# Sixteen rotating homes for the expert weights of a mixture-of-experts layer, with a staging buffer that VectorE fills

## The chip, the cores and the metric

The kernel runs on one core of one Trainium2 chip. The metric is the device time of one execution in microseconds (us). TensorE (PE in the profile) multiplies, VectorE (DVE) and ScalarE (ACT) work element by element, GpSimd (POOL) gathers and scatters rows by indirect DMA, SyncE (SP) issues the weight loads.

## The reference, cut to what matters

One layer of an encoder trunk: a matrix-memory branch and a latent-attention branch, merged, then a top-4-of-32 mixture of experts on 336 tokens of 1024 features, all in float32. The change lies in the mixture of experts:

```python
def moe(x2, w_router, b_router, w_gu, b_gu, w_dn, b_dn):
    logits = (x2 @ w_router).astype(jnp.float32) + b_router.astype(jnp.float32)
    top_v, top_i = lax.top_k(logits, TOP_K)
    gates = jax.nn.softmax(top_v, axis=-1)
    ...
    def expert_block(args):
        xb, e = args
        gu = xb @ w_gu[e] + b_gu[e]
        gate = jnp.minimum(gu[:, :D_FF], SWIGLU_LIMIT)
        up = jnp.clip(gu[:, D_FF:], -SWIGLU_LIMIT, SWIGLU_LIMIT)
        hid = (up + 1.0) * gate * jax.nn.sigmoid(SWIGLU_ALPHA * gate)
        return hid @ w_dn[e] + b_dn[e]
```

An expert's weights are 1024 x 2048 (gate and up) and 1024 x 1024 (down), together 12 MB. All 32 experts get tokens, so all 384 MB are read once.

## The kernel before, in words

The first 584 us do the two branches, the output projection and the router; the change only renames buffers there. From then on the kernel works in blocks of 64 token rows, each of one expert. With the given inputs there are 39 blocks: experts 8, 10, 18, 20 and 29 have two, expert 26 has three, the other 26 have one.

An expert's weights come as 12 pieces of 128 x 2048 float32 (1 MB): `up 0` to `up 7` (gate and up columns for 128 input rows each) and `down 0` to `down 3`. Each piece has a fixed place in the buffer `ring` (`up_w`, L360; `dn_w`, L369), so there is room for exactly one expert. SyncE loads them in a loop over experts (L568 to L577): piece k of the next expert is issued when TensorE has used piece k of this expert in this expert's last block (semaphores `m_up`, `m_down`; each piece's landing is counted in `up_in[k]`, `dn_in[j]`).

TensorE's loop (L1084 to L1103) is skewed by a block. An iteration b turns the tokens of block b+1 (L619, eight transposes), adds the biases (L1015), turns the hidden rows of block b (L619, four), and then takes the twelve pieces in the order up 0 (of block b+1), down 0, 1, 2 (of block b), up 1, down 3, up 2 to up 7 (L1025, L1031 are gate and up, L1051 is down). Each piece is four matmuls of 64 rows by 512 columns, each of which the profile lists as two. A pair, left columns then right columns, runs side by side in the two column halves of the array. VectorE's loop (L1848 to L1863) does the gated unit between up 7 and the turning of the hidden rows: clip gate (L1440), `pick` for the bias (L1440), clip up (L1440), multiply (L1443), `hid` (L1446). ScalarE does the sigmoid and the copies out of PSUM. GpSimd gathers the token rows (L1973) and scatters the results (L2001) for each block; down 0 of a block waits until the scatter of the block before has landed (`yrow_free`).

After the last block the twelve result pieces `y_turn` are loaded into `ring` and summed (L588 on).

Of the kernel before, what the change touches and what calls it, by code (L numbers as in the profile page):

```python
# [22 lines left out]
D = 1024  # L23
# [73 lines left out]
UPSLOT, DNSLOT = [4, 5, 3, 0], [1, 2]  # L97
# [103 lines left out]
def build(nc, i, o, x_rows_dram, y_rows_dram):  # L201
    with ExitStack() as ctx:
# [7 lines left out]
        ring = sb("ring", [128, 6 * SLOT])  # L210
        r_xt = sb("r_xt", [128, KD * NT])
        r_o = sb("r_o", [128, KD * NT])
        r_kv = sb("r_kv", [128, 3968])
        r_qk = sb("r_qk", [128, 16 * (NT + 3)])
        r_v = sb("r_v", [128, KD * NT])
# [5 lines left out]
        u_pad = sb("u_pad", [128, 2, NT + 6])  # L221
        sig = sb("sig", [128, 2, NT + 3])
# [9 lines left out]
        wrow = sb("wrow", [4, 2, NT])  # L232
        emat = sb("emat", [128, 2, NT])
        wib_hi = sb("wib_hi", [128, 2, NT])
# [5 lines left out]
        def r3(ap, a):  # L240
            return ap.rearrange("p (a b) -> p a b", a=a)

        ident = cst("ident")
        scratch = ring[:, 4 * SLOT:6 * SLOT]
# [7 lines left out]
        bd_rows = r_v[0:NE, 0:1024]  # L252
# [3 lines left out]
        oT = r3(ring[:, 3 * SLOT:3 * SLOT + KD * NT], KD)  # L256
# [46 lines left out]
        g_ffn_b = r_v[:, 1216:2240]  # L303
        g_fin_b = r_xt[:, 0:1024]
        w_rt = r3(r_xt[:, 1024:1280], KD)
# [38 lines left out]
        inslot = r3(r_kv[:, 0:12 * BLK], 12)  # L344
        inblk = r3(r_kv[:, 1536:1536 + 12 * NB1], 12)
        spread = r3(r_o[:, 384:384 + 12 * NB1], 12)
        prod = r_o[:, 0:384].rearrange("p (t k e) -> p t k e", t=3, k=4)
        cmp6 = r_v[:, 2240:2240 + NE * 6].rearrange("p (e n) -> p e n", n=6)

        xg = r3(r_kv[:, 0:512], 8)  # L350
        hidT = r3(r_kv[:, 512:1024], 4)
        gt = r_kv[:, 1024:1536]
        up = r_kv[:, 2048:2560]
        sg = r_o[:, 0:512]
        gateT = r_o[0:NE, 2048:2048 + NT]
        hid = r_v[:, 0:512]
        xrow = r_v[0:BLK, 1216:2240]
        yrow = r_xt[:, 1280:1792]

        def up_w(k):  # L360
            at = UPSLOT[k // 2] * SLOT + 2 * D * (k % 2)
            return ring[:, at:at + 2 * D]

        def y_turn(t, r):
            n = 3 * r + t
            at = 4 * SLOT + D * n if n < 8 else 3 * SLOT + D * (n - 8)
            return ring[0:ROWS[t][1], at:at + D]

        def dn_w(j):  # L369
            at = DNSLOT[j // 2] * SLOT + 2 * D * (j % 2)  # L370
            return ring[:, at:at + 2 * D].rearrange("p (s f) -> p s f", s=2)
# [19 lines left out]
        def taken(eng, *name):  # L391
# [8 lines left out]
            "ld_w_q", "xg_even", "xg_odd", "sq_odd", "sq_sum", "x_var", "x_root", "xt_ready"))  # L400
        ld_cache, ld_x1, ld_C, stored_kv = sem("ld_cache"), sem("ld_x1"), sem("ld_C"), sem("stored_kv")
# [30 lines left out]
        def pslot(slot, n):  # L432
            return ring[:, slot * SLOT:slot * SLOT + n]
# [42 lines left out]
        dn = i["w_down"][0].rearrange("e (j p s) f -> p e j (s f)", p=128, s=2)  # L476

# [4 lines left out]
        def _(sp):  # L482
# [65 lines left out]
            sp.dma_start(bd_rows, i["b_down"][0]).then_inc(ld_late, 16)  # L548
            for k in range(4):
                sp.dma_start(up_w(k), gu[:, 0, k, :]).then_inc(up_in[k], 16)  # L550
# [7 lines left out]
            sp.dma_start(g_fin_b, i["g_final_norm"].rearrange("(a d) -> a d", a=1).broadcast_to([128, D])  # L558
                         ).then_inc(ld_late, 16)
            filled(sp, "ya", 7)  # L560
            for k in range(4, 8):
                sp.dma_start(up_w(k), gu[:, 0, k, :]).then_inc(up_in[k], 16)
# [1505 lines left out]
```

## Time and profile before

| | us |
|---|---|
| median of three runs | 1660.77 (1659.41 to 1665.76) |
| the profiled execution's own time | 1667.29 |
| its span | 1665.5 |
| TensorE busy | 1524.4 (92%) |
| VectorE busy | 360.3 (22%) |
| ScalarE busy | 339.8 (20%) |
| GpSimd busy | 131.7 (8%) |
| granted TensorE clock, mean | 0.951 |

The busy shares are averages over the whole span. From 584 us on the DMA engines read weights at 410 to 420 GB/s in most of the page's 40 slices, with dips in some, and TensorE is busy 80 to 99% of a slice. So the experts' part has to be read in stretches: where TensorE waits for a weight piece, and where the DMA queue has nothing to do.

### The profile page before, as it was taken

The page shows a single profiled execution, that of the slowest core. Times are in us where ns is not written, and L with a number is a line of the kernel's source. Part 1 is how long each engine was busy: PE and PEld are TensorE (multiplying, and loading weights), DVE is VectorE, ACT ScalarE, POOL GpSimd, SP SyncE. Part 2 cuts the span into 40 slices and gives each one's busy share as a digit, 9 for nine tenths or more (in the row PEclk, how much of TensorE's full clock was granted, in tenths as well). Part 3 has the DMA queues.
Part 4 walks back from the last instruction along what each step waited for, and adds up shares of the span by engine and source line. Part 5 has one row for each costly group of instructions (what it writes and reads, how often), then busy time and mean ns, then how long its engine had stood idle before and what let it go on. Part 6 is the DMA issues. An engine that isn't in the chain of part 4 may idle for free.

```text
span 1665.5 us, 20381 instructions
## 1 busy us (share of the span) xinstructions
PE 1524.4 (92%) x7060; PEld 698.1 (42%) x7061; DVE 360.3 (22%) x860; ACT 339.8 (20%) x648; POOL 131.7 (8%) x237
## 2 busy tenths in 40 slices
PE   9999999999999998877899988788999887998994
PEld 6666666666665433222233332222333222333331
DVE  4664522423201511010011100100111010101015
ACT  4434323534101111110111111101111110111111
POOL 1100000000000000000001100000101000010010
PEclk9998999999999999988999998889999998999996
DMA  9121132212554389999989899999899999579897
GB/s 346 62 80 65 54 110 78 77 51 102 172 205 168 136 319 414 417 419 408 418 311 403 361 414 415 410 411 421 306 374 388 408 414 398 237 310 413 331 410 263
DMA packets 91398, 478.91 MB, mean 288 GB/s; under 512 B 12490, under 2 KB 15386, under 8 KB 41952
## 3 DMA queue, kind: packets, MB, share of 16 engines
q1 hardware_dynamic: 82976, 462.15, 69.8%
q0 software_dynamic: 8096, 16.04, 2.9%
q8 instruction: 22, 0.36, 0.1%
q10 hardware_dynamic: 288, 0.22, 0.1%
q14 instruction: 16, 0.13, 0.0%
HBM read 472.81 MB, written 15.51 MB: 293 GB/s over the span
## 4 chain that ended last, share of the span: by engine, by line
PE 73%; DMA 18%; DVE 4%; issue 3%; SPq 1%; ACT 1%; DVEq 0%; POOLq 0%; POOL 0%; ACTq 0%
PE bank L615 28%; PE bank L1025 21%; DMA ring<-in_w_gate_up 17%; PE bank L1051 17%; PE bank L619 2%; PE bank L1031 1%; DVE r_kv L1443 1%; DVE r_v L1446 1%; PE bank L874 1%; PE bank L642 1%; DVE r_c L1446 1%; SPq L569 0%; PE bank L748 0%; DVE r_qk L1440 0%; SPq L576 0%
## 5 line engine op out<-in xcount | busy, mean ns | idle before, releaser
L1025 PE MATMUL bank<-ring,r_kv 128*64 128x512 f32 x2184 | 517.6, 621 | 89.1 <-DMA ring<-in_w_gate_up 88.5
L1025 PEld LDWEIGHTS bank<-ring,r_kv 128*64 128x64 f32 x2184 | 156.3, 142 | 396.5 <-issue 301.4
L1051 PE MATMUL bank<-ring,r_kv 128*64 128x512 f32 x1248 | 292.5, 612 | 0.7 <-ACT r_kv L1135 0.7
L1440 DVE TENSOR_SCALAR r_kv<-bank 128x512 f32<-128x512 f32 x78 | 53.9, 692 | 916.3 <-PE bank L1031 916.1
L615 PE MATMUL bank<-r_xt,ring 128*128 128x336 f32 x768 | 227.6, 451 | 1.1 <-ACT r_o L1135 0.9
L1051 PEld LDWEIGHTS bank<-ring,r_kv 128*64 128x64 f32 x1248 | 93.4, 144 | 197.7 <-issue 196.6
L615 PEld LDWEIGHTS bank<-r_xt,ring 128*128 128x128 f32 x768 | 144.1, 191 | 70.7 <-issue 5.7
L1135 ACT ACTIVATE r_xt<-bank 128x512 f32<-128x512 f32 x39 | 23.3, 597 | 509.7 <-PE bank L1051 509.7
L1386 ACT ACTIVATE r_o<-r_kv 128x512 f32<-128x512 f32 x39 | 24.6, 631 | 318.4 <-DVE r_kv L1440 318.4
L615 PE MATMUL bank<-ring 128*128 128x336 f32 (+2 forms) x352 | 87.6, 432 | 0.0
L619 PEld LDWEIGHTS bank<-const,r_v 64*128 64x128 f32 (+3 forms) x524 | 49.3, 156 | 77.3 <-DVE r_v L1446 43.9
L619 PE MATMUL bank<-const,r_v 64*128 64x64 f32 (+3 forms) x524 | 63.8, 257 | 10.8 <-DVE r_v L1446 10.4
L1031 PE MATMUL bank<-ring,r_kv 128*64 128x512 f32 x312 | 73.5, 592 | 0.0
L1135 ACT ACTIVATE r_kv<-bank 128x512 f32<-128x512 f32 (+3 forms) x85 | 49.8, 586 | 92.7 <-PE bank L619 87.4
L615 PEld LDWEIGHTS bank<-ring 128*128 128x128 f32 (+2 forms) x352 | 57.1, 189 | 26.8 <-issue 2.8
L615 PE MATMUL bank<-ring,r_kv 128*128 128x128 f32 (+4 forms) x192 | 60.0, 449 | 1.2 <-DVE r_kv L1443 1.2
L1386 ACT ACT_TABLE_LOAD x39 | 50.0, 1283 | 12.6 <-ACT r_xt L1135 12.4
L1997 POOL COPY r_qk<-r_qk 128x1 uint32 x39 | 7.0, 180 | 557.1 <-ACT r_xt L1135 557.1
L1015 PE MATMUL bank<-bgu,r_qk 32*64 32x512 f32 x312 | 42.4, 612 | 9.1 <-DVE r_kv L1440 8.8
L615 PE MATMUL bank<-r_kv,ring 128*128 128x336 f32 (+9 forms) x192 | 44.4, 360 | 0.0
L1973 POOL DMA_INDIRECT r_v<-x_rows,r_qk x41 | 40.0, 976 | 47.3 <-POOL r_qk L1990 33.2
L615 PEld LDWEIGHTS bank<-ring,r_kv 128*128 128x128 f32 (+3 forms) x192 | 30.9, 186 | 29.1 <-issue 23.6
(251 smaller groups left out, 945.7 us busy)
## 6 DMA issues: line engine op xcount, KB each, us to landing
ring<-in_w_gate_up SPq DMA_DIRECT2D x256, 1024.0 KB, 18.0
ring<-in_w_down SPq DMA_DIRECT2D x128, 1024.0 KB, 14.9
ring<-in_w_in SPq DMA_DIRECT2D x12, 2048.0 KB, 7.7
ring<-in_w_proj_b SPq DMA_DIRECT2D x2, 2048.0 KB, 7.6
ring<-in_w_proj_a SPq DMA_DIRECT2D x2, 2048.0 KB, 9.3
ring<-in_w_out SPq DMA_DIRECT2D x2, 2048.0 KB, 7.7
ring<-y_rows SPq DMA_DIRECT2D x8, 512.0 KB, 8.7
ring<-in_first SPq DMA_DIRECT2D x4, 592.0 KB, 5.8
```

The source lines that it names most:

```text
L615: ins = pe.matmul(out, l, r, start=(n == 0), stop=(n == len(pairs) - 1), **kw)
L619: return pe.transpose(out, src, ident[0:src.shape[0], 0:src.shape[0]])
L642: ins = pe.matmul(low[n][:, 0:NT], w_first[:, k, 128 * n:128 * n + 128], xg_mix[:, k, :], start=(k == 0), stop=(k == KD - 1), skip_group_c ...
L1015: pe.matmul(half(gate_bank if q < 2 else up_bank, q % 2), pick[32 * q:32 * q + 32, :], bgu[32 * q:32 * q + 32, :], start=True, stop=False, ...
L1025: ins = pe.matmul(half(gate_bank if q < 2 else up_bank, q % 2), xg[:, k, :], w[:, 512 * q:512 * q + 512], start=False, stop=False, skip_gr ...
L1031: ins = pe.matmul(half(bank_, t), xg[:, 7, :], w[:, 512 * (q0 + t):512 * (q0 + t) + 512], start=False, stop=True, skip_group_check=True)
L1051: ins = pe.matmul(half(out_bank, t), hidT[:, 2 * (j % 2) + s, BLK * h:BLK * h + BLK], w[:, s, 512 * t:512 * t + 512], start=(j == 0 and s ...
L1135: return act.activation(out, src, ACT.Copy, scale=scale)
L1386: act.activation(sg, gt, ACT.Sigmoid, scale=ALPHA).then_inc(m_sig, 1)
L1440: return dve.tensor_scalar(out, a, s1, s2, op0, op1)
L1446: return dve.scalar_tensor_tensor(out=out, in0=a, scalar=s, in1=b, op0=op0, op1=op1)
L1973: pool.indirect_dma_start(xrow, None, x_rows_dram[:, :], bass.IndirectOffsetOnAxis(ap=column[0:BLK, :].bitcast(U32), axis=0), bounds_check ...
```

## The change

`ring` now has sixteen homes of one piece each instead of fixed places for twelve. Piece n of expert e (up 0 to 7 are 0 to 7, down 0 to 3 are 8 to 11) lies at home (12 e + n) mod 16, so the pattern repeats every four experts. SyncE's loop over experts is written out for four phases. A piece may be issued when the piece sixteen places earlier in the stream has been used: `up 0` to `up 3` of expert e wait for `down 0` to `down 3` of expert e-2, `up 4` on for `up 0` on of expert e-1. Each load also waits for the landing of the same piece of the expert before. Four pieces of expert 1 are issued before the block table is ready. The room comes from buffers of the first part (`r_xt`, `r_v`, `r_o`), whose later tenants move to `usig`, `rowt`, `r_qk`, `r_c` and `r_rt`.

Because a piece's home differs from expert to expert and TensorE's loop is one body for all blocks, the matmul on the left 512 columns reads its weights through a register; the right columns (1024 elements a partition and piece) are copied by VectorE from the home into one of four fixed buffers `stage`, and the other matmul reads there. TensorE waits for the copy (`staged`) in place of the landing; VectorE waits for the landing and, from the fifth copy of an iteration on, for TensorE's use of the piece four uses earlier.

```diff
-UPSLOT, DNSLOT = [4, 5, 3, 0], [1, 2]
+PIECE, HOMES = 2048, 16
+USE = [("up", 0), ("down", 0), ("down", 1), ("down", 2), ("up", 1), ("down", 3)] + [("up", k) for k in range(2, 8)]
+def home(e, n):
+    return (12 * e + n) % HOMES
...
+        def experts_of(eng, b):
+            e, e1 = (eng.value_load(bei[0:1, bass.ds(eng.snap(b + n), 1)].bitcast(I32), min_val=0, max_val=NE - 1)
+                     for n in (0, 1))
+            def four(expert, n):
+                return ring[:, bass.ds(eng.snap((3 * expert + n) % 4 * (4 * PIECE)), 4 * PIECE)]
+            return (None, None, four(e, 2)), (four(e1, 0), four(e1, 1)), e, e1
...
             for j in range(4):
-                sp.dma_start(dn_w(j).rearrange("p s f -> p (s f)"), dn[:, 0, j, :]).then_inc(dn_in[j], 16)
+                down_in(0, j, dn[:, 0, j, :])
+            for k in range(4):
+                if k == 2:
+                    filled(sp, "lg", 2)
+                sp.wait_ge(up_in[k], 16)
+                gate_up_in(1, k, gu[:, 1, k, :])
+            sp.wait_ge(x2_ready, 3)
+            sp.dma_start(g_fin_b, i["g_final_norm"].rearrange("(a d) -> a d", a=1).broadcast_to([128, D])
+                         ).then_inc(ld_fin, 16)
             sp.wait_ge(moe_tab, 1)
-            with sp.Fori(1, NE) as e:
-                before = sp.value_load(firsti[0:1, bass.ds(e, 1)].bitcast(I32), min_val=0, max_val=MAXB)
-                for k in range(8):
-                    sp.wait_ge(m_up, before * 8 + k + 1)
...
+            def expert_in(e, phase, first_k=0):
+                old, before = last_block(e - 2) if first_k == 0 else None, last_block(e - 1)
+                for k in range(first_k, 8):
+                    if k < 4:
+                        sp.wait_ge(m_down, old * 4 + k + 1)
+                    else:
+                        sp.wait_ge(m_up, before * 8 + k - 3)
+                    sp.wait_ge(up_in[k], 16 * e)
+                    gate_up_in(phase, k, gu[:, bass.ds(e, 1), k, :].rearrange("p a f -> p (a f)"))
                 for j in range(4):
+                    sp.wait_ge(m_up, before * 8 + j + 5)
+                    sp.wait_ge(dn_in[j], 16 * e)
+                    down_in(phase, j, dn[:, bass.ds(e, 1), j, :].rearrange("p a f -> p (a f)"))
...
+            def moving(fours, n, u):
+                w, s = fours[n // 4][:, PIECE * (n % 4):PIECE * (n % 4) + PIECE], stage[:, u % 4, :]
+                return [lambda g: w[:, 1024 * g:1024 * g + 512], lambda g: s[:, 512 * g:512 * g + 512]]
...
-                gate_up(0, e1)
...
+                for u, (kind, n) in enumerate(USE):
+                    if u == 1:
+                        pe.wait_ge(m_hidT, b + 1)
+                        pe.wait_ge(yrow_free, b + 1)
+                    pe.wait_ge(staged, 12 * b + u + 1)
...
+            def stage_right(b, u, own, new, e, e1):
+                kind, n = USE[u]
+                if kind == "up":
+                    dve.wait_ge(up_in[n], 16 * e1 + 16)
+                    src = new[n // 4]
+                else:
+                    dve.wait_ge(dn_in[n], 16 * e + 16)
+                    src = own[2]
+                if u >= 4:
+                    was, m = USE[u - 4]
...
+                src = r3(src[:, PIECE * (n % 4):PIECE * (n % 4) + PIECE], 4)[:, 1:4:2, :]
+                dve.tensor_copy(r3(stage[:, u % 4, :], 2), src).then_inc(staged, 1)
...
+            with dve.Fori(0, last) as b:
+                glu(b)
+                own, new, e, e1 = experts_of(dve, b)
+                for u in range(12):
+                    stage_right(b, u, own, new, e, e1)
```

How the instructions stand now. TensorE before, from the turning of the hidden rows to down 0 (L619 is the turn, L1025 is up 0, L1051 down 0; ISA is a register instruction):

```order
L619 MATMUL bank1<-const,r_v 128x128 [waits m_hid]
L619 MATMUL bank1<-const,r_v 128x128 x3
L1021 ISA [waits m_xg]
L1025 MATMUL bank2<-ring,r_kv 64x512 [waits up_in0]
L1025 MATMUL bank2<-ring,r_kv 64x512
L1025 MATMUL bank3<-ring,r_kv 64x512 x2
L1046 ISA [waits yrow_free,m_hidT]
L1051 MATMUL bank4<-ring,r_kv 64x512 [waits dn_in0]
L1051 MATMUL bank4<-ring,r_kv 64x512 x3
```

The same place now (L665 is the turn, L1070 up 0, L1104 down 0):

```order
L665 MATMUL bank1<-const,r_qk 128x128 [waits m_hid]
L665 MATMUL bank1<-const,r_qk 128x128 x3
L1151 ISA [waits m_xg]
L1070 ISA [waits staged]
L1070 MATMUL bank2<-ring,r_qk 64x512
L1070 MATMUL bank2<-stage,r_qk 64x512
L1070 ISA
L1070 MATMUL bank3<-ring,r_qk 64x512
L1070 MATMUL bank3<-stage,r_qk 64x512
L1151 REGISTER_ALU [waits yrow_free,m_hidT]
L1104 ISA [waits staged]
L1104 MATMUL bank4<-ring,r_qk 64x512
```

The matmuls are the same in number and order; each piece has gained two or three register instructions, and its wait is for the copy. VectorE's loop before, from the multiply to the loop's end (L1443 the multiply, L1446 `hid`):

```order
L1443 TENSOR_TENSOR r_kv<-r_kv,r_o 128x512 [waits m_gt,m_sig]
L1446 SCALAR_TENSOR_TENSOR r_v<-r_kv 128x512 [waits m_dve,m_read]
L1861 REGISTER_ALU [waits m_hid]
L1848 REGISTER_ALU [waits moe_tab,m_pick]
L1848 COMPARE_AND_BRANCH
```

The same place now, up to the second copy (L1496 the multiply, L1499 `hid`, L489 reads the two expert numbers, L1931 the copies):

```order
L1496 TENSOR_TENSOR r_qk<-r_qk 128x512 [waits m_gt,m_sig]
L1499 SCALAR_TENSOR_TENSOR r_qk<-r_qk 128x512 [waits m_dve,m_read]
L489 ISA
L489 TENSOR_LOAD r_qk
L489 ISA x3
L489 TENSOR_LOAD r_qk
L489 ISA x2
L1919 ISA
L1931 ISA [waits up_in0]
L1931 COPY stage<-ring 128x1024
L1922 ISA
L1931 ISA [waits dn_in0]
```

Two register loads, nine register instructions and twelve copies now stand behind `hid` in every iteration.

## Rows read from the trace of the kernel before

**Rows 1.** The page: share of the span of the chain that ended last.

```profile
PE 73%; DMA 18%; DVE 4%; issue 3%; SPq 1%; ACT 1%; DVEq 0%; POOLq 0%; POOL 0%; ACTq 0%
```

**Rows 2.** Timeline of TensorE: start, length; in brackets idle before and releaser.

```profile
626.06 1.89 PE L1031 MATMUL bank<-ring,r_kv 128*64 128x512 f32 x8
627.88 0.71 PE L619 MATMUL bank<-const,r_v 64*128 64x64 f32 x8
...
630.14 0.74 PE L619 MATMUL bank<-const,r_v 128*128 128x128 f32 x4 [0.23 <-DVE r_v L1446]
630.81 1.94 PE L1025 MATMUL bank<-ring,r_kv 128*64 128x512 f32 x8
632.58 5.32 PE L1051 MATMUL bank<-ring,r_kv 128*64 128x512 f32 x24
...
649.75 1.89 PE L1031 MATMUL bank<-ring,r_kv 128*64 128x512 f32 x8
...
1018.64 3.68 PE L1025 MATMUL bank<-ring,r_kv 128*64 128x512 f32 x8 [6.35 <-DMA ring<-in_w_gate_up]
1022.11 6.37 PE L1051 MATMUL bank<-ring,r_kv 128*64 128x512 f32 x24
...
1143.35 3.68 PE L1025 MATMUL bank<-ring,r_kv 128*64 128x512 f32 x8 [6.08 <-DMA ring<-in_w_gate_up]
```

**Rows 3.** TensorE's waits in 640 to 820, 970 to 1150, 1300 to 1415, 1520 to 1545.

```profile
PE bank L1025 <- DMA ring<-in_w_gate_up: 31.9, 6, 6.7
...
PE bank L1025 <- DMA ring<-in_w_gate_up: 31.2, 6, 6.7
...
PE bank L1025 <- DMA ring<-in_w_gate_up: 20.7, 4, 6.6
...
PE bank L1025 <- DMA ring<-in_w_gate_up: 4.8, 1, 4.8
```

**Rows 4.** Stretches: busy of each engine, granted clock, DMA share, GB/s.

```profile
940.00:980.00 40.00, 39.54 (x198) 13.74 (x194) 4.17 (x8) 6.21 (x8) 3.77 (x6) 1.00 1.02 418
...
1450.00:1490.00 40.00, 39.07 (x200) 13.84 (x198) 5.67 (x10) 5.53 (x8) 3.94 (x6) 1.00 0.59 230
```

**Rows 5.** Timeline of VectorE: `hid`, before the turning.

```profile
629.39 0.69 DVE L1446 SCALAR_TENSOR_TENSOR r_v<-r_kv 128x512 f32<-128x512 f32 x1
```

**Rows 6.** Register loads and register work on the queues: ns min/median/max, first and last start.

```profile
L1085 PEldq TENSOR_LOAD <-r_qk x38: 298/302/319, 600.0 to 1601.6; - x38
L1085 PEldq FUSED_REGOPS  x38: 151/151/156, 600.4 to 1601.9; - x38
L1846 DVEq TENSOR_LOAD <-r_qk x1: 546/546/546, 600.5 to 600.5; - x1
L1440 DVEq FUSED_REGOPS  x39: 57/57/65, 603.5 to 1628.4; - x39
```

**Rows 7.** Groups of VectorE by shape: busy us, mean ns | idle before.

```profile
L1446 DVE SCALAR_TENSOR_TENSOR r_c<-ring,r_qk,r_c 128x1024 f32<-128x1024 f32 x8 | 10.3, 1284 | 9.6 <-DMA ring<-y_rows 9.6
...
L1440 DVE TENSOR_SCALAR ring<-ring,st 128x576 f32<-128x576 f32 x4 | 2.1, 520 | 0.1
...
L1440 DVE TENSOR_SCALAR ring<-ring,st 128x144 f32<-128x144 f32 x4 | 1.2, 296 | 0.1
```

**Rows 8.** Timeline of TensorE: the first block, and the last.

```profile
582.58 0.71 PE L619 MATMUL bank<-const,r_v 64*128 64x64 f32 x8 [0.48 <-DMA r_v<-x_rows,r_qk]
583.97 1.94 PE L1025 MATMUL bank<-ring,r_kv 128*64 128x512 f32 x8 [0.69 <-ACT r_kv L1135]
...
1631.39 0.93 PE L619 MATMUL bank<-const,r_v 128*128 128x128 f32 x4 [1.55 <-DVE r_v L1446]
1633.02 9.85 PE L1051 MATMUL bank<-ring,r_kv 128*64 128x512 f32 x32 [0.69 <-ACT r_kv L1135]
```

**Rows 9.** GpSimd's gather: its place in the timeline, and issue to landing of all.

```profile
630.20 0.98 POOL L1973 DMA_INDIRECT r_v<-x_rows,r_qk  x1 [0.86 <-POOL r_qk L1990]
...
DMA to landing us min/median/max: 3.0/7.0/8.9
```

More of the change, by code:

```diff
@@ L207, in sem, with r3 @@
             return ctx.enter_context(nc.semaphore(name))
[L210 to L213, printed above, removed]
+        def r3(ap, a):
+            return ap.rearrange("p (a b) -> p a b", a=a)
+        ring = sb("ring", [128, HOMES * PIECE])
+        spare = ring[:, 12 * PIECE:HOMES * PIECE]
+        r_xt, r_v, r_o = (spare[:, KD * NT * n:KD * NT * (n + 1)] for n in range(3))
+        stage = sb("stage", [128, 4, 1024])
+        r_kv = stage[:, :, :].rearrange("p a b -> p (a b)")[:, 0:3968]
         r_qk = sb("r_qk", [128, 16 * (NT + 3)])
-        r_v = sb("r_v", [128, KD * NT])
+        r_rt = sb("r_rt", [128, 256])
         r_c = sb("r_c", [128, 4112])
@@ L578, in _ @@
+            expert_in(1, 1, 4)
+            expert_in(2, 2)
+            expert_in(3, 3)
+            with sp.Fori(0, NE // 4 - 1) as n:
+                for phase in range(4):
+                    expert_in(sp.snap(4 * n + 4 + phase), phase)
             nb = sp.value_load(nbi[0:1, 0:1].bitcast(I32), min_val=NE, max_val=MAXB)
@@ L1017, in bias, with gate_up @@
                               start=True, stop=False, skip_group_check=True)
-            def gate_up(k, e):
-                pe.wait_ge(up_in[k], 16 * e + 16)
-                w = up_w(k)
+            def gate_up(k, left, right):
+                parts = (left, right)
                 if k < 7:
@@ L1042, in hidden_turned, with down @@
                 ins.then_inc(m_turn, 1)
-            def down(j, e):
-                pe.wait_ge(dn_in[j], 16 * e + 16)
-                w = dn_w(j)
-                h = j // 2
+            def down(j, left, right):
+                h, parts = j // 2, (left, right)
                 for s in range(2):
@@ L1093, in _ @@
                 pe.wait_ge(m_xg, b + 2)
-                gate_up(0, e1)
-                pe.wait_ge(m_hidT, b + 1)
-                pe.wait_ge(yrow_free, b + 1)
-                down(0, e)
-                down(1, e)
-                down(2, e)
-                gate_up(1, e1)
-                down(3, e)
-                for k in range(2, 8):
-                    gate_up(k, e1)
+                for u, (kind, n) in enumerate(USE):
[4 more added lines that the diff above has]
+                    if kind == "up":
+                        gate_up(n, *moving(new, n, u))
+                    else:
+                        down(n, *moving(own, 8 + n, u))
             pe.wait_ge(m_xrow, 16 * nb + 16)
@@ L1110, in _ @@
             for j in range(4):
-                down(j, NE - 1)
+                pe.wait_ge(dn_in[j], 16 * NE)
+                down(j, *fixed(NE - 1, 8 + j))
         @block.scalar
@@ L1847, in _, with glu @@
             dve.wait_ge(moe_tab, 1)
-            with dve.Fori(0, nb) as b:
+            def glu(b):
                 dve.wait_ge(m_gate, b + 1)
@@ L1863, in _ @@
                 dve.nop()
+            glu(last)
+            dve.wait_ge(m_hid, nb)
+            dve.wait_ge(m_pick, nb + 1)
             def add_turn(t, r):
```

124 lines of the change are left out of this document (66 added, 58 removed).

## The prediction

> **What bounds the kernel now.** I read the page's chain first [rows 1]: TensorE holds 73% of it and DMA 18%, and that 18% is the part a weight buffer can touch. Then TensorE's timeline in the experts' part [rows 2]. It has two kinds of block. In one, up 7 at 626.06 is followed by up 7 at 649.75: a cycle of 23.69 us with no idle but 0.23 us ahead of the bias and of the turning. In the other, up 0 waits for its weights: 6.35 us at 1018.64. From that block to the one at 1143.35 there are four such cycles, 124.7 us, or 31.2 us each. That is the rate of the loads: 12 pieces in 31.2 us, 2.60 us a piece, with the block's own rows in it. So a block of TensorE is 7.5 us shorter than the load of an expert, and with one block per expert the loads bound.
>
> The waits lie in four stretches [rows 3]: 31.9, 31.2, 20.7 and 4.8 us, 88.6 in all in 17 waits. Between them come the experts with two or three blocks, where TensorE needs 47 or 71 us for one expert's weights, gets ahead of nothing, and the load queue runs dry because every place is taken. The stretch 1450 to 1490 shows it: TensorE at full clock, DMA share 0.59, 230 GB/s; from 940 to 980 the share is back at 1.02 [rows 4]. These dry times are what more room can win back.
>
> A wait costs more than itself. After the 6.35 us wait, up 0 takes 3.68 us where an undisturbed one takes 1.94, and down 0 to 2 take 6.37 where they take 5.32 [rows 2]: 2.8 us more. Up 0 at nearly twice its time is what the lower of the clock's two levels, 1.2 for 2.4 GHz, would give; after part of down 0 to 2 it is back. In a row of starved blocks this costs nothing (the next wait is shorter by as much), but where a wait goes altogether it goes too.
>
> **The gain: four more places.** Twelve pieces of room become sixteen. Each time the queue would have run dry, it now goes on for four pieces, 4 x 2.60 = 10.4 us. The stretch of waits behind it shrinks by that, since in it everything follows the loads. Three stretches have more than 10.4 us in them and shrink by 10.4 each, 31.2; the last has 4.8 us in one wait and goes with its 2.8 us of slow clock, 7.6. Sum: 38.8 us. This supposes that each dry time was at least 10.4 us long. For 1450 to 1490 it was more than that (0.41 x 40 = 16 us), and two double experts stand ahead of the other stretches, each leaving 2 x 23.7 - 31.2 = 16 us. The first stretch starts from an early start instead: four pieces of expert 1 are now in by about 584.
>
> **The cost on the path: VectorE behind `hid`.** Up 0 of the next block used to follow the turning directly, at 630.81 [rows 2]. Now it waits for the first copy, which stands behind `hid` (start 629.39 [rows 5]) and behind two register loads and the register work. TensorE's queue does such a load in 0.30 us, VectorE's only one took 0.55, its first; I take 0.34 for a repeated one. Register work right behind a load took 0.15 on TensorE, I take 0.2; five other register instructions at 0.057 and one or two longer ones make 0.35 [rows 6]. Together 2 x 0.34 + 2 x 0.2 + 0.35 = 1.43 us. TensorE's loads of a first iteration start at 600.0 [rows 6], while its matmuls of the block go on (a cycle ahead of 627.88, so to 604.2), so the queue works beside its engine; I let VectorE's start with `hid`. The copy then starts at 630.87.
>
> The copy's length is in no row. Two scalar operations in SBUF took 296 ns for 144 elements and 520 for 576, or 0.52 ns an element [rows 7]; carried to 1024 that is 0.75 us. An operation with two tensor inputs took 1.284 us for 1024, the upper bound; 0.52, a shorter copy of the same kind, is below. I take 0.75, the same kind. The copy ends at 631.62; with 0.1 for the signal and 0.05 for TensorE's register instruction, up 0 starts at 631.8 instead of 630.8. I charge 0.9 us a block, as the pieces behind it come sooner (a copy is 0.75 us, a piece 1.72 to 1.77 us of TensorE: the start of 632.58 less that of 630.81) and the copies of later pieces are hidden by the matmuls four uses ahead. Its bounds are 0 (if up 0 finds its copy ready) and 630.08 + 1.6 + 1.28 + 0.15 - 630.81 = 2.3 (queue work only behind `hid`, cold prices, full-length copy).
>
> Which blocks pay? In a stretch of waits none: the copy delays TensorE, not the loads, which have eight or more pieces queued. Nor do blocks ahead of a stretch once the queue is full again, for what they lose shortens the wait to come. Those that pay run from the end of a stretch to the time when the queue is full again: from 814 to about 955, six; from 1143, six; from 1410 to the end, nine, because nothing behind them collects it any more; and two at the start. 23 x 0.9 = 20.7 us.
>
> **The same in TensorE's queue.** Three more register instructions a piece, 0.06 each by VectorE's rows [rows 6]. They are hidden if the queue runs ahead as at 600.0, which the four-deep `stage` allows. I take 0; exposed they cost 0.14 us a piece.
>
> **The start.** The four early pieces and the final norm's gains are in flight when the first token rows are gathered, and TensorE already waits 0.48 us for these [rows 8]. Gathers land in 3.0 us at best and 7.0 in the median, beside weight loads [rows 9]. Between 0 and 4 us; I take 1, as most of the early load is over by then. SyncE's longer loop has the queued pieces as cover; renamed buffers ahead of 584 us and the tail cost nothing, having the same instructions.
>
> **Sum.** -38.8 + 20.7 + 1 = -17.1 us. On the profiled execution's 1667.3 that gives 1650; it stands 6.5 us above the median of the runs, so on 1660.8 it is 1644.
>
> **A rule that speaks against it.** In rows 9 GpSimd's gather occupies its engine from 630.20 to 631.18, and the first copy would start at 630.87 inside it. No row here shows VectorE's one-input SBUF operations beside such a gather. The Trainium skill ("SBUF — State Buffer", the section "SBUF: two separate sides") says that VectorE in a two-port mode, which a float32 copy in SBUF uses, and GpSimd hold their shared ports as an exclusive lock, and warns of descriptors delayed by such copies. By that rule the copy would wait until 631.2, 0.3 us a block, and the sum would be 7 us worse: 1651. The reverse, a gather held up by copies, has until the next turning of tokens, over 20 us later, to be late in.
>
> **The rivals.**
> A, the gain at little cost. The copy is found ready or nearly so, 0.2 us a block: -38.8 + 4.6 + 1, or 1628. For it: each price above is an estimate that may be high. Against: copies must stand behind `hid` in order. Chance 0.10.
> B, the gain is eaten. VectorE's queue starts its register work only when `hid` has ended (0.65 more), or the copy takes 1.28 us (0.5 more): 1.45 to 2.05 a block, -38.8 + 33 to 47 + 1, or 1656 to 1670. For it: all this is serial and nothing covers it. Against: rows 6 and 7. Chance 0.22.
> C, slower, TensorE's register work is exposed. Matmuls of a block come 0.14 us a piece late because the queue cannot run ahead past the wait on `staged`. 12 x 0.14 = 1.7 us a block besides the 0.9: 23 x 2.6 = 60, -38.8 + 60 + 1 = +22, or 1683. It decides from 0.07 us a piece on (21 / 23 / 12 = 0.08). Against: the waits at down 0 with a register instruction before it left no idle at 632.58 [rows 2]. Chance 0.07.
> D, slower, the clock. In the last block idles of 1.55 and 0.69 us around the turning were enough: 32 matmuls took 9.85 us where 24 take 5.32 undisturbed, so 7.1 were due. At the first block 0.48 and 0.69 were not enough: up 0 took 1.94 [rows 8, 2]. A block paced by TensorE would now have 0.23, 0.23 and 0.9. If that is enough, 23 x 2.8 = 64 more: 1708. Chance 0.06.
> E, slower, the homes don't help: the order of waits in SyncE's loop (landing of the same piece of the expert before, ahead of each load) keeps the queue as short as before. Then only costs are left, +21.7: 1682. Against: twelve pieces may still be in flight, 31 us. Chance 0.03.
>
> **How the numbers follow.** My forecast, 0.52. Half a per cent, 8 us, is about what a measurement can tell from no change; so "faster" is below 1652.5 and "slower" above 1669. Faster: forecast and A, 0.62. Same: B, 0.22. Slower: C, D, E, 0.16. The forecast alone runs from 1634 (0.45 us a block) to 1652 (1.25). The range reaches from 1624, below A, to 1672, over B's upper end, which leaves out C, D and E and a little of A's.
>
> **What the changed profile would show.** The waits of TensorE on landing become waits on VectorE's copy; starved blocks fall from 17 to 13 or 14, still 31.2 us apart. The dry stretches shorten; around 1535 there is none. In blocks paced by TensorE the cycle is 24.4 to 24.8 us, with an idle of 0.7 to 1.1 before up 0 and 1.94 for up 0 itself. The copies take 0.7 to 0.8 us each, VectorE is busy some 340 us more. I am wrong if the cycle exceeds 25.3 us, if up 0 runs at the lower clock after a short idle, if starved blocks are further apart than 31.2 us, or if a gap shows up between pieces later in a block.

## Result, and the profile after

The changed kernel takes 1658.15 us (median of 20 runs, 1650.98 to 1662.14), the kernel before 1666.57 beside it (20 runs, 1659.41 to 1674.38). The ratio is 0.9943, with a 95% interval from 0.9926 to 0.996: 9.5 us less, or 7 to 12; the medians differ by 8.4. The forecast was 17.1 us less on its own base, about twice the gain. That base was the median of three runs, 1660.8, which stands 5.8 us below the median of twenty, so the changes are compared here and not the times. Direction and range hold; the two cost terms, VectorE behind `hid` and the start, do not. The profiled execution has a span of 1654.4 us (own time 1656.31).

The page's chain first, the row that answers to [rows 1], and the engines' totals:

```profile
PE 1508.4 (91%) x7060; PEld 699.8 (42%) x7061; DVE 667.0 (40%) x1317; ACT 339.6 (21%) x648; POOL 147.9 (9%) x237
...
PE 69%; DMA 18%; DVE 5%; issue 4%; DVEq 2%; ACT 1%; SPq 0%; POOL 0%; POOLq 0%; ACTq 0%
```

VectorE's queue (DVEq: register loads and register arithmetic, which its engine doesn't count as busy) held 0% of the chain and holds 2%, or some 33 us.

TensorE's waits, in the stretches 650 to 820, 820 to 970, 970 to 1150, 1150 to 1300, 1300 to 1415, 1415 to 1530 and 1530 to 1660: in total, times, longest. They answer to [rows 3]:

```profile
PE bank L1070 <- DVE stage L1931: 24.9, 6, 6.8
...
PE bank L1070 <- DVE stage L1931: 7.1, 6, 1.2
...
PE bank L1070 <- DVE stage L1931: 23.5, 6, 6.5
...
PE bank L1070 <- DVE stage L1931: 7.1, 6, 1.2
...
PE bank L1070 <- DVE stage L1931: 15.2, 4, 9.0
...
PE bank L1070 <- DVE stage L1931: 5.9, 5, 1.2
...
PE bank L1070 <- DVE stage L1931: 3.5, 3, 1.2
```

Every up 0 but the first now waits, and always for a copy. In 28 of them the wait is 1.2 us; in ten it is longer, since the copy itself waits for weights. I call a block whose weights are late a starved one: 17 of them have become ten, and the one near 1535 is gone. TensorE's timeline, one block paced by TensorE and one that is starved (start, length; in brackets the idle before and who ended it), against [rows 2]:

```profile
929.70 1.09 PE L1061 MATMUL bank<-bgu,r_qk 32*64 32x512 f32 x8 [0.23 <-DVE r_qk L1493]
931.02 0.75 PE L665 MATMUL bank<-const,r_qk 128*128 128x128 f32 x4 [0.23 <-DVE r_qk L1499]
932.94 0.64 PE L1070 MATMUL bank<-ring,r_qk 128*64 x1 [1.18 <-DVE stage L1931]
...
957.89 0.64 PE L1070 MATMUL bank<-ring,r_qk 128*64 x1 [1.20 <-DVE stage L1931]
...
1037.99 1.11 PE L1070 MATMUL bank<-ring,r_qk 128*64 x1 [6.49 <-DVE stage L1931]
```

The cycle is 957.89 - 932.94 = 24.95 us (24.93 in most blocks) for 23.69: 1.24 us more, all of it between the turning and up 0 (932.94 - 931.02 = 1.92 us from start to start, for 0.67 in [rows 2]). A first matmul of 0.64 us after an idle of 1.18 is the higher clock, 1.11 after 6.49 the lower. Between the pieces later in the block there is no gap. The starved blocks of the first stretch lie (805.48 - 712.40) / 3 = 31.0 us apart, as before.

VectorE and GpSimd around the same turning (against [rows 5] and [rows 9]), and then, from the chain of waits, VectorE's queue in between (start, length):

```profile
930.27 0.69 DVE L1499 SCALAR_TENSOR_TENSOR r_qk<-r_qk 128x512 f32<-128x512 f32 x1
931.06 0.97 POOL L2056 DMA_INDIRECT usig<-x_rows,r_qk  x1 [0.85 <-POOL r_qk L2073]
...
932.04 2.50 DVE L1931 COPY stage<-ring 128x1024 f32 x4 [1.08 <-issue]
```

```profile
930.39 0.31 DVEq L489
930.70 0.04 issue
930.74 0.19 DVEq L489
930.93 0.03 issue
...
931.13 0.30 DVEq L489
931.43 0.03 issue
931.47 0.20 DVEq L489
...
931.86 0.14 DVEq L1931
932.00 0.04 issue
```

The queue work begins with `hid`, as supposed, and runs 1.65 us; `hid` covers 0.57 of it, and VectorE then idles 1.08. The copy starts 1.77 us after `hid` started. Two more things are seen here and taken up below: the copy starts 0.01 us after the gather has ended, and queue instructions have a gap of 0.03 to 0.05 us between them.

The dry stretch of [rows 4] has shrunk: from 1450 to 1490 the DMA share is 0.84 for 0.59, and from 820 to 860 it is 0.99 for 0.82.

```profile
820.00:860.00 40.00, 36.71 (x190) 13.25 (x188) 17.61 (x28) 6.59 (x9) 5.92 (x7) 1.00 0.99 398
...
1450.00:1490.00 40.00, 38.37 (x190) 13.64 (x188) 16.67 (x26) 5.59 (x7) 4.73 (x6) 1.00 0.84 322
```

The start, against [rows 8]:

```profile
578.04 0.71 PE L665 MATMUL bank<-const,usig 64*128 64x64 f32 x8 [2.80 <-DMA usig<-x_rows,r_qk]
579.44 3.43 PE L1070 MATMUL bank<-ring,r_qk 128*64 128x512 f32 x8 [0.69 <-ACT r_qk L1188]
```

TensorE waits 2.80 us for the first token rows instead of 0.48, and up 0 then takes 3.43 us instead of 1.94.

**Which part of the profiles' difference is chance.** The spans differ by 11.1 us, and 6.3 of that has nothing to do with the change. After an idle of 1.4 us at 134 us the clock sometimes stays up and sometimes falls (from 140 to 150 us the granted clock is 0.50 in the profile before and 1.00 in the one after). The next idle of 0.44 us then comes 65 us later or 58.7; the work between is of the same kind in both kernels:

```profile
134.87 1.13 PE L615 MATMUL bank<-ring,r_c 128*128 128x128 f32 x8 [1.41 <-ACT ring L1135]
199.86 1.13 PE L615 MATMUL bank<-ring,r_c 128*128 128x128 f32 x8 [0.44 <-ACT ring L1135]
```

```profile
134.23 1.13 PE L661 MATMUL bank<-ring,r_c 128*128 128x128 f32 x8 [1.40 <-ACT ring L1188]
192.89 1.13 PE L661 MATMUL bank<-ring,r_c 128*128 128x128 f32 x8 [0.44 <-ACT ring L1188]
```

The first pair is of the kernel before, the second of the changed one. So profiles are compared below over the experts' part alone, from up 0 of the first block to the last turning: 1047.4 us before (1631.39 - 583.97), 1041.8 after (1621.21 - 579.44), and terms are weighed by the ratios of many runs.

### The profile page after: what moved, and what is told of

It reads as the page before. It is cut to its first block, busy times and chain, and to the rows that moved or that the text cites. A ratio compares the mean times of both kernels' runs of the same rounds, so it can differ in the third digit from the quotient of the medians.

```text
span 1654.4 us, 23723 instructions
## 1 busy us (share of the span) xinstructions
PE 1508.4 (91%) x7060; PEld 699.8 (42%) x7061; DVE 667.0 (40%) x1317; ACT 339.6 (21%) x648; POOL 147.9 (9%) x237
## 4 chain that ended last, share of the span: by engine, by line
PE 69%; DMA 18%; DVE 5%; issue 4%; DVEq 2%; ACT 1%; SPq 0%; POOL 0%; POOLq 0%; ACTq 0%
PE bank L661 28%; PE bank L1070 23%; DMA ring<-in_w_gate_up 17%; PE bank L1104 13%; DVEq L489 2%; DVE stage L1931 2%; PE bank L665 2%; PE bank L1076 1%; DVE r_qk L1496 1%; DVE r_qk L1493 1%; PE bank L920 1%; DVE r_c L1499 1%; PE bank L688 1%; PE bank L794 0%; PE bank L915 0%
## 5 line engine op out<-in xcount | busy, mean ns | idle before, releaser
L1070 PE MATMUL bank<-ring,r_qk 128*64 (+1 forms) x1120 | 510.2, 617 | 90.2 <-DVE stage L1931 89.6
L1070 PE MATMUL bank<-stage,r_qk 128*64 128x512 f32 x1064 | 494.3, 612 | 0.0
L1931 DVE COPY stage<-ring 128x1024 f32 x456 | 306.6, 693 | 414.1 <-PE bank L1104 154.3
L661 PE MATMUL bank<-ring 128*128 128x336 f32 x1248 | 347.6, 444 | 1.1 <-ACT ring L1188 0.9
L1070 PEld LDWEIGHTS bank<-ring,r_qk 128*64 128x64 f32 x1120 | 149.8, 141 | 391.8 <-issue 391.0
L1104 PE MATMUL bank<-ring,r_qk 128*64 (+1 forms) x640 | 289.4, 611 | 0.7 <-ACT r_qk L1188 0.7
L1104 PE MATMUL bank<-stage,r_qk 128*64 128x512 f32 x608 | 280.5, 605 | 0.0
L661 PEld LDWEIGHTS bank<-ring 128*128 128x128 f32 x1248 | 224.3, 190 | 109.1 <-issue 8.9
L1104 PEld LDWEIGHTS bank<-ring,r_qk 128*64 128x64 f32 x640 | 88.7, 142 | 189.2 <-issue 188.3
L1070 PEld LDWEIGHTS bank<-stage,r_qk 128*64 128x64 f32 x1064 | 145.7, 140 | 0.0
L1493 DVE TENSOR_SCALAR r_qk<-bank 128x512 f32<-128x512 f32 (+1 forms) x79 | 54.2, 686 | 186.8 <-PE bank L1076 186.5
L1104 PEld LDWEIGHTS bank<-stage,r_qk 128*64 128x64 f32 x608 | 86.2, 142 | 0.0
L1076 PE MATMUL bank<-ring,r_qk 128*64 (+1 forms) x160 | 73.3, 592 | 0.0
L1076 PE MATMUL bank<-stage,r_qk 128*64 128x512 f32 x152 | 71.4, 592 | 0.0
L661 PE MATMUL bank<-ring,stage 128*128 128x128 f32 (+4 forms) x192 | 59.2, 445 | 1.2 <-DVE stage L1496 1.2
L2084 POOL DMA_INDIRECT y_rows<-r_c,r_qk x39 | 55.6, 1426 | 34.4 <-POOL r_qk L2080 34.4
L1188 ACT ACTIVATE ring<-bank 128x64 f32<-128x64 f32 (+12 forms) x110 | 38.8, 352 | 68.3 <-PE bank L661 34.0
## 6 DMA issues: line engine op xcount, KB each, us to landing
ring<-in_w_gate_up SPq DMA_DIRECT2D x256, 1024.0 KB, 19.0
ring<-in_w_down SPq DMA_DIRECT2D x128, 1024.0 KB, 21.9
```

Source lines behind the costliest of these rows:

```text
L661: ins = pe.matmul(out, l, r, start=(n == 0), stop=(n == len(pairs) - 1), **kw)
L1070: ins = pe.matmul(half(gate_bank if q < 2 else up_bank, q % 2), xg[:, k, :], parts[q % 2](q // 2), start=False, stop=False, skip_group_che ...
L1076: ins = pe.matmul(half(bank_, t), xg[:, 7, :], parts[t](g), start=False, stop=True, skip_group_check=True)
L1104: ins = pe.matmul(half(out_bank, t), hidT[:, 2 * (j % 2) + s, BLK * h:BLK * h + BLK], parts[t](s), start=(j == 0 and s == 0), stop=(j == 3 ...
L1188: return act.activation(out, src, ACT.Copy, scale=scale)
L1493: return dve.tensor_scalar(out, a, s1, s2, op0, op1)
```

## Experiments

Ratios are to the kernel before, timed beside each; at 1670 us, 0.001 is 1.67 us.

**VectorE's loads first.**

```
             with dve.Fori(0, last) as b:
-                glu(b)
                 own, new, e, e1 = experts_of(dve, b)
+                glu(b)
```

> VectorE's two loads of expert numbers, with their register work, stand ahead of the block's first wait, not behind hid. Theory Q (queue work): in the changed kernel they run from 930.39 to 932.00 in a row on VectorE's queue and alone make the first copy late; now the copy starts at once behind hid, 1.0 us sooner. A block paced by TensorE then takes 23.9 to 24.0 us for 24.93, and with some 22 blocks that pay the time falls by 20 us or more, to about 1637 where the changed kernel has 1658. Rival L (shared port): in the changed kernel GpSimd's gather of the next rows runs from 931.06 to 932.03 and the copy starts at 932.04. If the copy is held until the gather has ended, it starts where it did, the cycle stays at 24.9 and the time at 1658.

Measured: 1639.53 us, ratio 0.9823 (0.9793 to 0.9854). Theory Q holds, and L falls: against the changed kernel's ratio this is 0.0120 or 20.0 us less. The timeline, at the same place:

```profile
930.65 0.69 DVE L1499 SCALAR_TENSOR_TENSOR r_qk<-r_qk 128x512 f32<-128x512 f32 x1
931.26 2.62 DVE L1931 COPY stage<-ring 128x1024 f32 x4
931.44 1.35 POOL L2056 DMA_INDIRECT usig<-x_rows,r_qk  x1 [0.85 <-POOL r_qk L2073]
...
932.15 0.64 PE L1070 MATMUL bank<-ring,r_qk 128*64 x1
...
955.90 0.64 PE L1070 MATMUL bank<-ring,r_qk 128*64 x1
```

The copy starts at once behind `hid`, the cycle is 955.90 - 932.15 = 23.75 us, and up 0 has no idle ahead of it. The copies run on beside the gather and are not held up; it is the gather that grows, from 0.97 to 1.35 us. Start and end together in the changed kernel were a coincidence. The experts' part takes 1606.81 - 587.18 = 1019.6 us, 22.1 less than in the changed kernel. At 1.18 us a block that is 19 blocks that pay, not 23; by the second profile of the changed kernel, below, it is 17. Up to the last starved block of each row the two profiles differ by 2.5, 6.3 and 3.7 us, and behind the last row by 9.7: about 2, 5, 3 and 8 blocks, for 2, 6, 6 and 9 forecast. And 13 blocks starve here, for ten with the loads behind `hid`.

**And copy 0 ahead of the gate work.**

```
-                glu(b)
-                for u in range(12):
+                glu(b, lambda: [stage_right(b, u, own, new, e, e1) for u in range(EARLY)])
+                for u in range(EARLY, 12):
```

(`EARLY` is 1, and `glu` calls the function first; the copy waits until up 4 is done with its buffer.)

> As the run with the loads first, and also the first of the twelve copies of a block is made ahead of the block's gate work, while TensorE is still on up 5 to up 7; VectorE idles 5.2 us there. Theory Q: up 0 finds its copy ready, the cycle is that of the kernel before, 23.69 us, and the time is some 6 us below the run with the loads first, about 1631. In blocks that wait for weights the copy now holds back the gate work, so the serial work behind the landing grows by 3 to 4 us there; since these blocks are paced by loads, it costs nothing in a row of them and at most 4 us at the end of each of the two or three stretches. Rival W: it costs there each time, and the time is no better than the run with the loads first, or up to 20 us worse.

Measured: 1644.18 us, ratio 0.9855 (0.982 to 0.9889), so 4.6 us above the run with the loads first where 6 below was expected; the intervals of the two ratios overlap. The cycle of a block paced by TensorE is 23.7 us as forecast. But the landing now holds back bias, gate work and turning, which used to lie beside the wait:

```profile
1038.31 0.69 DVE L1935 COPY stage<-ring 128x1024 f32 x1 [9.92 <-DMA ring<-in_w_gate_up]
...
1040.49 1.98 PE L1062 MATMUL bank<-bgu,r_qk 32*64 32x512 f32 x8 [5.45 <-DVE r_qk L1494]
...
1042.41 1.13 PE L666 MATMUL bank<-const,r_qk 128*128 128x128 f32 x4
```

Up 0 comes over 5 us after the landing, part of it at the lower clock, for 0.9 with the copy behind `hid`. The experts' part is 1611.74 - 587.73 = 1024.0, 4.4 more. So W holds and not Q. By the two profiles it loses 2.2, 0.6 and 1.4 us up to the first block behind each row of starved ones, and nothing behind the last.

**Twelve pieces ahead.**

```
                 for k in range(first_k, 8):
-                    if k < 4:
-                        sp.wait_ge(m_down, old * 4 + k + 1)
-                    else:
-                        sp.wait_ge(m_up, before * 8 + k - 3)
+                    sp.wait_ge(m_up, before * 8 + k + 1)
...
-                    sp.wait_ge(m_up, before * 8 + j + 5)
+                    sp.wait_ge(m_down, before * 4 + j + 1)
```

> The changed kernel with its copies and sixteen homes, but each load waits until TensorE is done with the same piece of the expert before, so at most twelve pieces are ahead, as in the kernel before. It measures the copies' cost alone. Theory H (each of the dry times gives back 10.4 us, a block costs 1.25): the gain of 31 to 39 us goes, and only the cost is left, 22 blocks of 1.25 us or 28 us over the kernel before, some 1694 us; a little less since the four early pieces of expert 1 stay, say 1685 to 1695. Rival N: the homes gave little, and the net gain came from the part ahead of the experts: 1660 to 1675.

Measured: 1698.18 us, ratio 1.0175 (1.0141 to 1.0209). H holds: 0.0175 is 29 us above the kernel before, for 28. The changed kernel's 0.9943 lies 0.0232 or 38.7 us (some 6 either way) below this, the gain of the four places; the forecast said 38.8. The profiles say 1657.51 - 580.19 = 1077.3 against 1041.8, 35.5. The wait near 1535 is back:

```profile
1557.72 1.11 PE L1067 MATMUL bank<-ring,r_qk 128*64 x1 [4.60 <-DVE stage L1928]
```

**Twelve ahead and the loads first**, both edits above together.

> At most twelve pieces ahead, as in that run before, and VectorE's two loads of expert numbers ahead of the block's first wait: the right halves are still copied. Theory Q (all of a block's cost is the queue work behind hid, the copies themselves cost nothing): the cycle is 23.75 us, 24 paying blocks are 1.18 us shorter, and of the 28 us that the copies cost nothing is left but the slower start, 1670 to 1675. Rival M (the copies' traffic in the on-chip memory also slows weight loads or the starved blocks): 1680 or more.

Measured: 1680.9 us, ratio 1.0061 (1.0038 to 1.0084). That is outside Q's range and just inside M's. Taking away the queue work gives 0.0114 or 19 us; 10 us (6 to 14) stay against the kernel before. So the change has a price besides the queue work. M's own cause does not show: within the three rows of starved blocks these lie 31.4, 31.2 and 31.4 us apart, and 31.2, 31.3 and 31.2 in the kernel before, so the loads are not slower. A part of the price is in view. The first copy stands behind the landing in a starved block, so up 0 starts 0.9 us after the copy does (in the run with the loads first the copy starts at 1036.75, up 0 at 1037.65), and what the last block of a stretch loses nobody collects: four times 0.9, or 3.6. A cycle of 23.75 for 23.69 is 1.4 in 23 blocks. The start, below, is 3 to 6. Together that is an estimate of 8 to 11 of the 10; the parts were not measured one by one.

**No early pieces.**

```
-            for k in range(4):
-                if k == 2:
-                    filled(sp, "lg", 2)
-                sp.wait_ge(up_in[k], 16)
-                gate_up_in(1, k, gu[:, 1, k, :])
+            filled(sp, "lg", 2)
...
+            for k in range(4):
+                sp.wait_ge(up_in[k], 16)
+                gate_up_in(1, k, gu[:, 1, k, :])
             expert_in(1, 1, 4)
```

> Up 0 to up 3 of expert 1 are loaded only once the tables are set, like all that follow, and not in front of them. In the changed kernel TensorE waited 2.80 us for the first token rows and then did up 0 of the first block in 3.43 us. Theory G: this is the price of the early loads. Without them the wait is 0.5 us, up 0 takes 1.94, the first block ends some 5 us sooner, but the first row of starved blocks is up to 10.4 us longer: the time is 3 to 8 us above the changed kernel. Rival P: the wait has another cause (the gathered rows land late whatever is loaded), stays at 2 us or more, and the time is 8 to 11 us above.

Measured: 1665.61 us, ratio 0.9964 (0.9939 to 0.9988), or 3.5 us above the changed kernel's. The time is in G's range, but its mechanism falls as it was put: the wait did not shrink, it grew.

```profile
588.97 1.11 PE L664 MATMUL bank<-const,usig 64*128 64x64 f32 x8 [5.36 <-DMA usig<-x_rows,r_qk]
```

But the edit had moved the loads onto the gather: the queue issues them at 580.53, the gather goes at 580.99. In the changed kernel, too, weights are in flight when the gather goes, at 572.62; in the kernel before they are not. The stretch 570 to 575 of the changed kernel, and then two of the kernel before, whose gather goes at 579.48 (second to last number: DMA share):

```profile
570.00:575.00 5.00, 4.74 (x36) 1.94 (x32) 3.72 (x13) 0.00 (x0) 1.03 (x1) 1.00 1.02 431
```

```profile
570.00:575.00 5.00, 5.00 (x9) 2.06 (x8) 4.55 (x14) 0.00 (x0) 0.00 (x0) 0.63 0.51 184
...
575.00:580.00 5.00, 4.69 (x60) 2.53 (x59) 3.77 (x16) 0.00 (x0) 0.52 (x1) 1.00 0.00 0
```

So the gather of the first rows may be late because bulk loads are in flight beside it. That made the next theory.

**Two pieces early, two behind the first rows**, with the loads first.

```
-            for k in range(4):
-                if k == 2:
-                    filled(sp, "lg", 2)
+            for k in range(2):
                 sp.wait_ge(up_in[k], 16)
                 gate_up_in(1, k, gu[:, 1, k, :])
+            filled(sp, "lg", 2)
...
+            sp.wait_ge(moe_tab, 1)
+            sp.wait_ge(m_gath, 1)
+            for k in range(2, 4):
+                sp.wait_ge(up_in[k], 16)
+                gate_up_in(1, k, gu[:, 1, k, :])
```

(The final norm's gains follow behind these.)

> The run with the loads first, and only up 0 and up 1 of expert 1 go out ahead of the tables; up 2, up 3 and the final norm's gains go out once the first token rows are turned. In the changed kernel the DMA share is 1.02 from 570 to 575, the gather issued at 572.62 lands 5.4 us later, while in the kernel before the share had fallen to 0.00 by its issue at 579.48 and it landed in 3.0. Theory B (bandwidth: the gather shares the DMA engines with weights in flight): TensorE's wait is 0.5 us again, up 0 of the first block takes 1.94 for 3.43, block 0 is 4 to 6 us shorter from the wait on, and since nothing else would have used the engines there, the time falls by 3 to 6 us to about 1635. Rival P (the gather lands late because its rows have just been stored, or by its place in the program): the wait stays above 2 us and the time does not move.

Measured: 1636.68 us, ratio 0.9781 (0.975 to 0.9811), the fastest version of all: 36.6 us below the kernel before. B's mechanism holds, P falls:

```profile
584.18 0.71 PE L668 MATMUL bank<-const,usig 64*128 64x64 f32 x8 [0.40 <-DMA usig<-x_rows,r_qk]
585.58 1.94 PE L1073 MATMUL bank<-ring,r_qk 128*64 128x512 f32 x8 [0.69 <-ACT r_qk L1191]
```

The wait is 3.05 us shorter than with the loads first, and the experts' part 2.8 (1602.41 - 585.58 = 1016.8): 5.9 together. The ratios differ by 0.0042 or 7.0 us and the medians by 2.9; with intervals as wide as these the times alone would not settle it.

**The same start in the changed kernel.**

> The changed kernel with the new order of the start alone: up 2, up 3 and the final norm's gains only once the first token rows are turned. VectorE's loads stay behind hid. The start's own share of the difference to the kernel before is read from it. Theory B (bandwidth): wait for the first rows 0.3 to 0.5 us for 2.80, up 0 of the first block 1.94 us for 3.43, and the time 4 to 6 us below the changed kernel, some 1653, a ratio of about 0.991 to the kernel before. Rival K (in the changed kernel the first stretch of waits takes the lost time back, so a quicker start only lengthens its first wait): within 2 us of the changed kernel.

Measured: 1656.59 us, ratio 0.9928 (0.9903 to 0.9953), 2.5 us below the changed kernel's ratio, within what the intervals allow for none. Wait and up 0 are as B says (0.41 and 1.94), the total lies between B and K. The second profile of the changed kernel is within 0.1 us of this one up to 565. Its first rows are turned at 580.63, here at 579.24; its up 0 takes 3.37 us, here 1.94; its last turning is at 1621.12, here at 1618.17. So all of 1.4 + 1.4 us is kept, 2.95 in the end. But the two profiles of the changed kernel differ by 2.7 us in their experts' parts, and the pair with the loads first gave 5.9. I take 3 to 6 us for the start; no run fixes it better.

**The loads twice.**

```
+                experts_of(dve, b)
                 own, new, e, e1 = experts_of(dve, b)
```

> The changed kernel with VectorE's two loads of expert numbers and their register work made twice behind hid, 1.3 us more of queue work, nothing else. It counts the blocks that pay. The cycle of a block paced by TensorE rises from 24.93 to 26.2 us. Theory F (the runs with the loads first show 18 paying blocks: 20 to 22 us for 1.18 a block): the time rises by 18 to 20 x 1.3, 24 to 26 us, to 1682 or so. Rival T (the 23 blocks of the forecast pay): 30 us, 1688. Rival Z (nearly all 39 blocks pay, since the starved ones have it behind the landing too): 50 us.

Measured: 1718.26 us, ratio 1.0292 (1.0258 to 1.0326), 58 us above the changed kernel: above all three theories (Z, the nearest, said 50), and the count of paying blocks can't be read from it. The idle ahead of up 0 rose by 1.25 us as expected, to 2.43. The cycle rose by more:

```profile
843.80 0.90 PE L1070 MATMUL bank<-ring,r_qk 128*64 x1 [2.43 <-DVE stage L1931]
...
871.67 1.11 PE L1070 MATMUL bank<-ring,r_qk 128*64 x1 [2.43 <-DVE stage L1931]
```

871.67 - 843.80 = 27.87 us, 2.94 more than 24.93, with 1.25 of idle. The rest is TensorE at its lower level: 1.11 for the first matmul is 1.2 GHz, 0.64 is 2.4. The forecast's rival D is this run; at 1.18 us of idle it was not there, at 2.43 it is. So of 2.94 us a block 1.69, over half the price of this edit, go with the clock.

**The kernel before, and the changed one, once more.**

> The kernel before again, for a second profile. In the first one TensorE's idle of 1.41 us at 134 us was followed by a lower clock, and the work up to the next idle of 0.44 us took 64.99 us; in the profile of the changed kernel, whose instructions there are of the same kinds and number, 58.66. If this is chance and has nothing to do with the change, some profiles of either kernel show the one and some the other, as three of the four runs made so far from the changed kernel show 65 us or more. The waits of the experts' part are as in the first profile within 1 us a stretch.

> The changed kernel again, for a second profile, with the same purpose: the experts' part from up 0 of the first block to the last turning takes 1041.8 us within 2 us, whatever the part ahead of it does.

Measured: 1670.04 and 1655.66 us. The first again shows 64.98 us from the idle at 134 to the next, the second 60.21. Of the ten profiles of the changed kernel and of versions of it, five have 64.9 to 66.5, two 60.2 and three 58.7, though their work there is the same; so it is chance there. That both profiles of the kernel before have the long one is too few to say whether it meets it more often. The experts' parts are 1634.46 - 583.85 = 1050.6 us before, and 1621.12 - 582.03 = 1039.1 after, each about 3 us from its first profile, more than the 2 expected of the second; two stretches of waits of the kernel before differ by 2 and 3 us from [rows 3], more than the 1 expected. Their means differ by 8.6 us.

## Why the prediction was wrong in size

Three differences of ratios part the change: from the kernel before to twelve ahead with the loads first, then the four places, then the loads put behind `hid`: 10.2 - 39.7 + 20.0 = -9.5 us. They share their runs, so that the sum comes out is no test; each term is good to 4 to 7 us. Against the forecast's -38.8 + 20.7 + 1:

- **The bound, and the gain of four places: right.** 39.7 us by this pair and 38.7 by the other. By the profiles of the first pair, row by row, it is 11.1, 10.4, 7.3 and 8.2 us, for 10.4, 10.4, 10.4 and 7.6. The starved blocks stay 31.0 us apart, the last single wait goes, the dry time from 1450 fills from 0.59 to 0.84.
- **The number of starved blocks:** 13 to 14 forecast, ten found. A block that pays 1.24 us also shortens the wait to come by it; the forecast used this for the cost and forgot it in the count. With the loads first, where blocks pay next to nothing, 13 starve.
- **The step that failed: "the cost on the path: VectorE behind `hid`", 0.9 us in 23 blocks and nothing in a stretch of waits.** This term was too small: price and last blocks were put too low, the count too high. The price of a block is 1.24. From `hid` to the copy it takes 1.77 us for 1.43: the instructions themselves are 1.30, less than forecast, but the first starts 0.12 after `hid`, and the gaps between them, which the forecast left out, make 0.35. The copy is 0.69 for 0.75, and the signal 0.20 for 0.15. (The prediction's 630.87 should read 629.39 + 1.43 = 630.82; its 0.9 goes with the latter.) The number is 17 to 19, not 23, and most of the difference lies ahead of the third row, three blocks for six. Why is argued and not tried apart: with sixteen places there is less dry time, the queue is full again sooner (from 1140 to 1180 the DMA share is 1.00 for 0.81 before), and what is lost from then on is collected by the next wait. And "in a stretch of waits none" is false for its last block, where the copy stands behind the landing: 0.9 each time. In all the queue work costs 20.0 us, and what else comes with the copies 4 to 7 (10.2 less the start): 24 to 27 us for 20.7.
- **The start: 3 to 6 us for 1.** "Most of the early load is over by then" was wrong: the share was 1.02 as the gather went. Its 5.4 us from issue at 572.62 to TensorE at 578.04 lie inside the bounds given; that up 0 behind the longer wait runs at the lower clock for a time, 3.43 us for 1.94, was not in them.
- **The other rivals.** The time lies among those of B, 1656 to 1670, but neither of B's causes is there: the queue work starts at 930.39, 0.12 after `hid`, and the copy takes 0.69 us. **TensorE's register work** (C): no gap between pieces, nothing exposed. **The clock** (D): up 0's first matmul takes 0.64 after 1.18 us of idle. **No help from the homes** (E): refuted by 39 us. The signs named ahead were nearly met: a cycle of 24.93 us for 24.4 to 24.8, an idle of 1.18 for 0.7 to 1.1, VectorE busy 307 us more for 340.
- **The rule of two sides of the on-chip memory.** The copy did begin only as the gather ended, as the Trainium skill's rule ("SBUF — State Buffer", "SBUF: two separate sides") would have it, yet for another reason. With the loads first, three copies run beside one gather: four copies take 2.62 us together for 2.50, while the gather takes 1.35 for 0.97. So most of the price falls on GpSimd, where it is hidden, and neither is shut out for the whole length of the other's instruction, as the rule puts it. The 7 us reckoned by it do not show: with copies and gather side by side the cycle is 23.75 us for 23.69.

So the gain was sized well. The two costs, 24 to 27 us for 20.7 and 3 to 6 for 1, left 9.5 us of the 17.1.

## What to carry to other kernels

Two register loads with their arithmetic held a queue for 1.65 us; in front of a wait that is there anyway they cost next to nothing (a cycle of 23.75 us for 23.69), behind the last operation of a chain 1.18 us a block (20 us here, for one moved line). When a buffer is fed earlier, look at what else is on the DMA engines just then: a small transfer that the chain waits for should not share them with bulk. And a cost on the path of a load-bound loop is paid neither by all blocks nor by none: count the blocks between the end of a row of waits and the time when the load queue is full again, and add the last of each row.

## What the runs showed of the hardware

- An idle of TensorE of 1.18 us a block left its clock at the higher level in all 28 blocks that had it; one of some 2.4 us, with the loads twice, brought the lower one in every block that had it, at the first matmul or within 1.1 us behind it, and then 1.25 us more idle cost 2.9. A first matmul of 0.64 is no proof that the clock stays: behind idles of 2.07 and 2.80 us in the run with the loads first it fell 0.9 and 1.3 us later (matmuls of 0.99 and 1.06), while behind one of 2.35 us at 1005.75 it did not fall. At 134 us one and the same idle of 1.4 us went both ways from run to run: what follows took 58.7 us in three profiles of the changed kernel and its versions, 60.2 in two and 64.9 to 66.5 in five.
- A float32 copy of 128 x 1024 in the on-chip memory takes 0.69 us, no more than a two-input operation on 512 elements. Beside such copies GpSimd's gather takes longer (its spans are rough in these profiles, but the same instruction is compared): the gathers from 600 to 1600 us average 976 ns in the changed kernel, where the copies start behind them, and 1225 with the loads first. Its scatters went from 1025 ns to 1417:

```profile
L2001 POOL DMA_INDIRECT y_rows<-r_xt,r_qk x37 | 37.9, 1025 | 32.7 <-POOL r_qk L1997 32.7
```

```profile
L2084 POOL DMA_INDIRECT y_rows<-r_c,r_qk x37 | 52.4, 1417 | 32.6 <-POOL r_qk L2080 32.6
L2056 POOL DMA_INDIRECT usig<-x_rows,r_qk x38 | 37.1, 976 | 32.4 <-POOL r_qk L2073 32.4
```

```profile
L2084 POOL DMA_INDIRECT y_rows<-r_c,r_qk x38 | 53.5, 1409 | 33.5 <-POOL r_qk L2080 33.5
L2056 POOL DMA_INDIRECT usig<-x_rows,r_qk x38 | 46.5, 1225 | 32.4 <-POOL r_qk L2073 32.4
```

The first is of the kernel before, the second of the changed kernel, the third of the run with the loads first (count, busy us, mean ns). That the scatters' growth is the copies' doing was not tried apart.

- A gather of token rows beside bulk loads lands later. From its issue to the start of the waiting turning it took 5.42 us in the changed kernel (DMA share 1.02 from 570 to 575) and 7.98 with no early pieces, where four pieces were issued 0.46 us ahead of it; with the engines free (share 0.00) it took 3.10 in the kernel before and 3.01 in the version with two pieces early.
